# First modulation in two halves of the features, with projection work between them, and x loaded first

## What is computed

```python
def modulation(c, w, b):
    return jnp.split(jax.nn.silu(c) @ w + b, 3, axis=-1)

def sandwich(x, mod, g_pre, g_post, fn):
    shift, scale, gate = mod
    h = rms_norm(x, g_pre) * (1.0 + scale[:, None]) + shift[:, None]
    return x + gate[:, None] * rms_norm(fn(h), g_post)
...
u, qr, fr, vr, gr = jnp.split(h @ hyb_w_in[j], split_at, axis=-1)
```

## Time and profile before

| | us |
|---|---|
| median of three runs | 1368.7 |
| lowest and highest run | 1366.57, 1370.73 |
| the profiled execution | 1364.06 |
| its span in the trace | 1362.3 |

### The profile page before, as it was taken

How to read it: one execution, slowest core, us unless ns; L and a number is a source line. 1 busy time by engine, 2 the same in 40 slices (tenths; PEclk the granted TensorE clock), 3 DMA queues, 4 the chain that set the end, 5 groups by cost and what they waited for, 6 DMA issues and landing times.

```text
span 1362.3 us, 22480 instructions
## 1 busy us (share of the span) xinstructions
PE 1337.2 (98%) x8896; PEld 1210.6 (89%) x8896; DVE 867.1 (64%) x1135; ACT 721.1 (53%) x1070; POOL 50.2 (4%) x76
## 2 busy tenths in 40 slices
PE   9999899999999999999999999999999998999999
PEld 8998699999789879999999899889999896899997
DVE  5788878886798557555565666564455567644554
ACT  3575554444644456444456663655555666655553
POOL 0101000000111000000001000000000000000000
PEclk7899899999899998999999999999999999999999
DMA  9978679985599633555555443355555542355540
GB/s 351 332 294 285 225 241 314 309 309 187 201 353 364 220 65 124 186 185 185 187 183 191 155 161 124 125 185 186 186 188 187 180 165 79 126 190 193 185 154 31
DMA packets 146337, 275.54 MB, mean 202 GB/s; under 512 B 4727, under 2 KB 83343, under 8 KB 146136
## 3 DMA queue, kind: packets, MB, share of 16 engines
q1 hardware_dynamic: 131152, 220.21, 47.9%
q0 software_dynamic: 13872, 52.05, 11.4%
q10 hardware_dynamic: 1240, 2.26, 0.5%
HBM read 273.40 MB, written 1.10 MB: 202 GB/s over the span
## 4 chain that ended last, share of the span: by engine, by line
PE 92%; DVE 4%; ACT 2%; issue 1%; DMA 1%; ACTq 0%; DVEq 0%
PE ps L1946 89%; PE ps L2084 1%; DVE acc_a L1193 1%; DVE wlo L1180 1%; PE ps L2315 1%; DMA ada_ring<-in_ada_w 1%; ACT whi L504 1%; DVE xn L1294 0%; ACT xn L558 0%; PE ps L2415 0%; DVE x L1281 0%; DVE h L1273 0%; DVE x L1288 0%; ACT small L565 0%; DVE hlo L1880 0%
## 5 line engine op out<-in xcount | busy, mean ns | idle before, releaser
L1180 DVE TENSOR_TENSOR wlo<-raw,whi 128x1024 fp32r<-128x1024 f32 x400 | 485.5, 1223 | 363.0 <-ACT whi L504 361.9
L504 ACT CAST whi<-raw 128x1024 fp32r<-128x1024 f32 x400 | 417.6, 1051 | 479.6 <-PE ps L1946 471.0
L1946 PE MATMUL ps<-hhi,whi 128*128 128x256 f32 x1792 | 507.0, 283 | 2.0 <-DVE hlo L1341 1.6
L1946 PE MATMUL ps<-hhi,wlo 128*128 128x256 f32 x1792 | 500.5, 279 | 0.0
L1946 PE MATMUL ps<-hlo,whi 128*128 128x256 f32 x1792 | 500.0, 279 | 0.0
L1946 PEld LDWEIGHTS ps<-hhi,whi 128*128 128x128 f32 x1792 | 336.1, 188 | 7.7 <-issue 5.1
L1946 PEld LDWEIGHTS ps<-hlo,whi 128*128 128x128 f32 x1792 | 336.1, 188 | 4.5 <-issue 2.2
L1946 PEld LDWEIGHTS ps<-hhi,wlo 128*128 128x128 f32 x1792 | 336.5, 188 | 0.0
L1946 PE MATMUL ps<-whi,hidhi 128*128 128x512 f32 x432 | 170.3, 394 | 0.0
L1946 PE MATMUL ps<-wlo,hidhi 128*128 128x512 f32 x432 | 169.1, 391 | 0.0
L1946 PE MATMUL ps<-whi,hidlo 128*128 128x512 f32 x432 | 168.7, 391 | 0.0
(11 more groups left out here) (234 smaller groups left out, 1181.9 us busy)
## 6 DMA issues: line engine op xcount, KB each, us to landing
raw<-in_ffn_w_in SPq DMA_DIRECT2D x44, 1024.0 KB, 6.0
ada_ring<-in_ada_w POOLq DMA_DIRECT2D x40, 1024.0 KB, 7.1
raw<-in_w_mlp_up SPq DMA_DIRECT2D x32, 1024.0 KB, 5.4
raw<-in_w_mlp_down SPq DMA_DIRECT2D x32, 1024.0 KB, 4.9
raw<-in_ffn_w_out SPq DMA_DIRECT2D x22, 1024.0 KB, 4.9
raw<-in_att_w_qkv SPq DMA_DIRECT2D x18, 1024.0 KB, 6.4
raw<-in_w_in_even SPq DMA_DIRECT2D x18, 1024.0 KB, 5.0
raw<-in_hyb_w_in SPq DMA_DIRECT2D x10, 1024.0 KB, 9.7
```

What stands on the lines that cost most here:

```text
L504: A.copy(whi[:, H % 4, :], raw[:, slot(n), h * HALF:(h + 1) * HALF]).then_inc(s["hi_ready"], 1)
L1180: V.tensor_tensor(wlo[:, H % 4, :], raw[:, slot(n), h * HALF:(h + 1) * HALF], whi[:, H % 4, :].bitcast(F32), ALU.subtract).then_inc(s["lo_ ...
L1946: return pe.matmul(out, lhsT, rhs, start=first, stop=last, skip_group_check=True)
```

## The change

Four things are different.

1. SP loads x first, then modulation loads 0 to 3, then the first 512 rows of projection blocks 0 and 1, then modulation loads 4 to 7, then the other rows of the two blocks. The modulation loads are put in another order of columns, so that the first four hold shift and scale of features 0 to 511, and the other four those of features 512 to 1023. The positions in the ring of slots follow (`ADA_POS`, `HYB_POS`).
2. `mod_first(0)` forms shift and scale of features 0 to 511 after four loads. ACT and DVE then make chunks 0 to 3 of `h`, and TensorE does halves 0 and 1 of blocks 0 and 1. Modulation loads 4 to 7 are worked on between these, then `mod_first(1)` forms the other features, and halves 2 and 3 of both blocks follow. The blocks now lie in PSUM banks 0 and 4, the third in 2, since two blocks are open at a time; the column sums move to banks 2 and 3.
3. On ACT the norms of x and the normalised x come ahead of the copies of the tables, and the three constant loads (`masks`, `bandqk`, `poolw`) ahead of the chunks of the second half of the features. On DVE `mean_x` comes ahead of the modulation.
4. On TensorE the transposes move from behind the sixth modulation load to behind the third, and the number of warm-up products is another at each place (`warm_cols` is `warm_ones` into another bank).

The core of the diff:

```diff
+            if b in (1, 2):
+                return (4, 2)[b - 1]
...
+        ADA_POS, HYB_POS = (0, 1, 2, 3, 6, 7, 8, 9), (4, 5, 10, 11)
...
+            def vacated(p):
+
+                if p in ADA_POS:
+                    sp.wait_ge(s["ada_used"], ADA_POS.index(p) + 1)
+                    sp.wait_ge(s["ada_pe"], ADA_POS.index(p) + 1)
+                elif p >= 0:
+                    sp.wait_ge(s["lo_ready"], 2 * HYB_POS.index(p) + 2)
...
-            for a in range(ADA_FIRST):
-                load(a - ADA_FIRST, 0, src_cols(t["ada_w"][0, 0], (a // 2) * 512, a % 2))
-                if a == 3:
-                    sp.dma_start(x[:, :, :], t["x"][0].rearrange("(t p) n -> p t n", p=P)).then_inc(s["x_in"], 16)
-            proj(FIRST["hyb_in"], t["hyb_w_in"][0], HYB)
+            sp.dma_start(x[:, :, :], t["x"][0].rearrange("(t p) n -> p t n", p=P)).then_inc(s["x_in"], 16)
+            for a in range(4):
+                load_ada(a)
+            for b in range(2):
+                load(b, 0, src_cols(t["hyb_w_in"][0], HYB[b][1], 0))
+            for a in range(4, ADA_FIRST):
+                load_ada(a)
+            for b in range(2):
+                load(2 + b, 0, src_cols(t["hyb_w_in"][0], HYB[b][1], 1))
+            proj(FIRST["hyb_in"] + 4, t["hyb_w_in"][0], HYB[2:])
...
+            mean_x(0, 0)
+            mean_x(0, 1)
             for a in range(4):
                 ada_first(a)
-            mean_x(0, 0)
-            mean_x(0, 1)
-            for a in range(4, ADA_FIRST):
-                ada_first(a)
-            mod_cols(0, 0)
+            mod_first(0)
+            shifted(0, 1)
             split(0)
-            pre(0)
+            low(0, 0)
+            low(0, 1)
+            shifted(0, 3)
+            split(1)
+            low(0, 2)
+            low(0, 3)
+            ada_first(4)
+            split(2)
+            ada_first(5)
+            split(3)
+            ada_first(6)
+            ada_first(7)
+            split(4)
+            mod_first(1)
...
-            for a in range(1, ADA_FIRST):
-                ada_cols(a)
-                warm_ones(2)
-                if a in (3, 5):
-                    add_cols(a // 2 - 1)
-                if a == 5:
-                    pe.wait_ge(s["vec_dil_c"], 4)
-                    turn(0)
-                if a == 6:
-                    add_cols(2)
+            warm_ones(4)
+            ada_cols(1)
+            warm_ones(4)
+            add_cols(0)
+            ada_cols(2)
+            pe.wait_ge(s["vec_dil_c"], 4)
+            turn(0)
+            ada_cols(3)
+            warm_ones(6)
+            add_cols(1)
+            warm_ones(12)
+            for h in range(2):
+                proj_half(HYB[0][0], pair_of(0), h, h, 0, 0)
+            ada_cols(4)
+            proj_half(HYB[1][0], pair_of(1), 2, 0)
+            ada_cols(5)
+            add_cols(2)
+            proj_half(HYB[1][0], pair_of(1), 3, 1)
+            ada_cols(6)
+            ada_cols(7)
+            warm_cols(4)
             add_cols(3)
-            warm_ones(12)
-
-            proj("hyb_in", HYB[0:2], j=0)
+            warm_cols(8)
+            for h in range(2, 4):
+                proj_half(HYB[0][0], pair_of(0), h + 2, h, 0, 0)
+            for h in range(2, 4):
+                proj_half(HYB[1][0], pair_of(1), h + 4, h)
```

More of the change, by code:

```diff
@@ L619, in pre @@
+                    chunk(j, k)
                     for H in splits_after(j, k):
@@ L687, in _ @@
             act.wait_ge(s["one_ready"], 1)
+            norms(0)
+            for tt, lo, hi in ((0, 0, D), (1, 0, 256), (1, 256, D)):
+                act.wait_ge(s["root_x"], tt + 1)
+                act.wait_ge(s["ssq_x"], 2 * tt + 2)
+                A.activation(xn1[:, tt, lo:hi], x[:, tt, lo:hi], ACT.Copy,
+                             scale=small[:, 5, 3 + tt:4 + tt]).then_inc(s["xn_ready"], 1)
             for g in range(3):
@@ L715, in _ @@
             act.dma_start(poolw[:, :, :], t["pool_w"][0].rearrange("g c d -> c g d")).then_inc(s["band_in"], 16)
+            split(4)
+            split(5)
+            act.wait_ge(s["mod_ready"], 2)
+            for i in range(4, KD):
+                chunk(0, i)
+            for H in range(6, 10):
+                split(H)
+            evac(0, 6, *HYB[0][::2], f1, tok1)
+            split(10)
+            split(11)
+            evac(1, 8, *HYB[1][::2], f1, tok1)
             fl = f1[:, :, :].rearrange("p a b -> p (a b)")
-            for b in range(3):
-                proj("hyb_in", HYB[b:b + 1], f1, tok1, b)
+            for b in range(1, 3):
+                if b == 2:
+                    proj("hyb_in", HYB[b:b + 1], f1, tok1, b)
                 if b == 1:
@@ new lines, in low @@
+            def low(j, k):
+                lo, hi = hlo[:, k, :], hhi[:, k, :].bitcast(F32)
+                if j < 4:
+                    dve.wait_ge(s["hhi_ready"], 8 * j + k + 1)
+                    V.tensor_tensor(lo, h32_slot(j, k), hi, ALU.subtract).then_inc(s["hlo_ready"], 1)
+                else:
+                    dve.wait_ge(s["hhi_ready"], 8 * j + bank_last(j, k) + 1)
+                    V.scalar_tensor_tensor(out=lo, in0=turned_ps(j, k), scalar=scol[:, j, k:k + 1], in1=hi,
+                                           op0=ALU.mult, op1=ALU.subtract).then_inc(s["hlo_ready"], 1)
@@ L2155, in warm_ones, with warm_cols @@
                     mm(ps[:, 1, 0:P], ones[:, :], ones[:, :])
+            def warm_cols(n):
+                for _ in range(n):
+                    mm(ps[:, 2, 2 * P:3 * P], ones[:, :], ones[:, :])
             def ada_cols(a):
-                pe.wait_ge(raw_in[a % RAW], 16 * (a // RAW + 1))
+                ada_raw_in(pe, a)
                 for kk in ada_direct(a):
```

144 lines of the change are left out of this document (85 added, 59 removed).

## The result

The change makes the kernel slower by half a per cent. Over 20 runs of each side, its median is 1374.66 us against 1368.21 us, and the ratio is 1.0048 with a 95% interval of 1.0035 to 1.006. The forecast was 1369.2 in a range of 1362.5 to 1376.0. The range holds the result, but the likeliest case (no measurable change) does not: the kernel came 5.5 us later than it said and lost by more than 0.3%. As a difference to the kernel before, +0.5 us was forecast and +6.45 measured.

What follows compares the result with a forecast made beforehand. It took TensorE's own list of small work, partly at half clock, as the bound. Terms of -1.5, +1 (gate weights) and +1 (clock fall) gave +0.5 us on the median 1368.7: 1369.2, range 1362.5 to 1376.

Steps and rivals of the forecast that it cites:

- the likeliest case: Whole kernel: no change beyond about 0.3% (4.1 us) against before; chance 0.52.
- The path is TensorE's list: First 66 us: TensorE's own gapless list of small work, not the loads, sets the time.
- Comes back with the transposes: Early stretch: clock falls behind the table products, returns to full with the transposes; block two ends 64.45 against 65.98.
- Rival (b): Early stretch: only the twelve warm-ups restore the clock, not the transposes; +3.2 us, +5.2 with allowances; chance 0.17.
- Idle time ahead of the first group, 1.74 us: TensorE at 8.96: waits for the first modulation load, now usable at 10.70; 0 to 1.74 us, taken as 1.74.
- rival (c): Start: new idle time at 8.96 drops the clock before the table products; +3.6 us, about +5.6 with allowances; chance 0.08.
- Gate weights, "I allow 1": Behind block two: gate weights begin some 3 us before its end, lateness partly covered; 0 to 6 us, allowed 1.
- the ring: Gate-weight loads behind block two: each later load is requested when its buffer is read, so late use delays later loads.
- rival (d): Block two's end to 120: late gate weights make VectorE, then TensorE, wait; +5 to +6 us; chance 0.05.
- The clock behind the fourth half, "I allow 1": Low groups after the fourth half: the clock may fall there; nothing up to 2.5 us, allowed 1.
- The sum: Whole kernel: -1.5 early, +1 gate weights, +1 clock fall gives +0.5 us, put on the median: 1369.2.

Runs made afterwards that it cites:

- second execution of before: The kernel before, unchanged, profiled once more: 1368.72 us.
- second execution of after: The kernel after, unchanged, profiled once more: 1373.08 us.
- part 3: Two runs on start idle time: x loaded first in the kernel before, ratio 1.0057; 30 start warm-up products instead of 24 in the kernel after, 1.0006.
- early gate weights: Kernel after with the first gate loads requested after the fourth modulation load and used earlier on VectorE: 1373.31 us, ratio 1.0038.
- the pair of executions at their medians: Both kernels unchanged, one profiled execution each, near their medians: before 1368.72 us, after 1374.64 us.
- moved gate block: Without the 14 warm-up products, 30 at the start, first gate block ahead of ninth and tenth low halves, against the kernel after: 1362.67 us, ratio 0.9976.

## Why the prediction was right and wrong

- **The path is TensorE's list: right.** The early times of the profiled execution follow from counts and the two levels of the clock, and its only other idle time up to block two's end is 0.23 us, for VectorE, ahead of the fifth half. A slip of reading did no harm: 0.67 in 16:17 puts the first fall at 16.3, not at 16.7, and the time at half clock before is 23.9 us, so up to 12 us lost, not 11.
- **"Comes back with the transposes": wrong, the step that failed early.** Rival (b), which held against it, gave first columns at 33.64, first projection 38.76 and block two's end 69.2. Measured are 34.31, 38.43 and 69.53, and half clock at 32 was its sign. That the last two agree so closely is partly luck: the columns came 0.7 later, the clock rose before the end of the twelve warm-up products and saved 1.0, and the rest took 0.6 longer. The forecast gave it 0.17 because the trace showed a rise at 33.4. The error was to read a rule from one rise in one execution. Of the 14 profiled executions of all versions, the clock came back inside the transposes or within 0.7 us of their end in seven, stayed at half past them in six, and had not fallen in one. The Trainium skill ("TensorE: Matmul & The Clock Gate", Part 4: PE-mode transpose) says that the full clock doesn't engage for products in transpose mode. Six of these executions fit it, but seven speak against it, if these transposes run in that mode, which the record does not say. What decides between the two stays open.
- **Idle time ahead of the first group, 1.74 us: about right in size (1.53), wrong in weight.** It was priced as time only, with 0.08 for rival (c), the clock falling with it. That fall came in three of the four profiled executions with an idle time of 1.4 us or more (1.93, 1.44 and 1.98, not 1.53), and in none of the ten others, five of them with 0.79 to 1.27 and five with none. The three are also executions whose warm-up products went over to full speed early (last section). But so are the second execution of before, with no idle time there, and two of those with 30 products at the start (0.83 and 0.84 us). These had no such fall, so the idle time is the likelier cause. By the medians of part 3 the start is worth some 6 us in either direction.
- **Gate weights, "I allow 1": too small, and the largest miss.** The start of the first gate block was right ("some 3 us ahead of the end", measured 3.2). What was wrong is that its lateness would be covered. It cost 2.15 us by level 1 (3.25 - 1.10) and some 1.5 of the 2.4 more by the second transposes, so 3.6 to 4.5 us in place of 1. The rows that the prediction read end at 110, and it weighed only the wait of 1.30 in them. Further on, in the same trace of before, the ring makes VectorE wait 4.09 and 0.81 us (at 126.44 and 130.10), so a delay there is not covered. The upper bound of 6 us held. The sign of rival (d), idle time of TensorE ended by VectorE between block two and 120, came (1.99 us at level 1). Its price of 5 to 6 us, given 0.05, is nearer to the measured one than the allowance of 1.
- **The clock behind the fourth half, "I allow 1": about right.** It cost nothing in the first execution of after and 1.1 us in the second. Its upper bound of 2.5 was nearly right too: 2.7 in one execution with the early gate weights. With late loads on top it cost 7.6 us (block two's end 70.30 against 59.81, less the 2.85 by which the first projection was later already), which no bound of the prediction held.
- **The sum.** It put the difference, +0.5, on the median of before as if both kernels drew the same early clock. By the pair of executions at their medians, block two's end is +1.1 and not -1.5, the fall behind the fourth half is 0 and not +1, and what follows, most of it the ring, is +4.5 and not +1. That gives 5.6 of the 6.45 us measured. That the range held the result owes to its width, which took in the rivals. The halves themselves seem to win: x first alone costs 4 us at block two's end, the whole change only 1.1. This is not shown. It is a difference of single executions, whose clock paths alone move block two's end by 2.5 us, and no run had the halves without x first.

## What to carry to other kernels

A ring that asks for its next load when the last is read turns a late first use into a late chain, so count what each later load waits for before moving that use, and do not ask early where the same DMA engines carry loads that are due sooner. Fill idle time ahead of small work with products that cost nothing there, and try the kernel without them where they lie on the path. Before a rise or a fall of the clock is given a cause, look at a second execution.

## What the runs showed that was not expected

- The clock's path is not fixed by the program. With the same code, the kernel before was first back at full at 33.4 in one execution and at 45.3 in another; the kernel after at 37.4 in one, and at 14.9 and again at 28.5 in the other (the first rise, during the warm-up products of the start, is not counted here). The Trainium skill ("TensorE: Matmul & The Clock Gate", Part 1) says that the same kernel shows different counts of slow products at its start from run to run. The runs here agree, and show it for the later falls and rises too, at a cost of microseconds; the prediction had not weighed it.
- The 24 warm-up products of the start end at 8.96 in one execution of before and 8.15 in another (start of the next row), though the granted clock reads 1.00 in all windows from 1.5 us on in both. The counts of rows show what the clock column does not: TensorE has 6 or 7 rows in a window of 1 us at first and 11 to 13 later. The count is 11 from 6:7 on in the one and from 5:6 on (9 in 4:5) in the other, so the start runs at about half speed in both, and for longer in the one. Why the turn comes at another time stays open. With an early end the wait for the first load is longer, and the three executions whose clock fell at once are among those with an early turn.
- Between the second and the third transposes the list takes 197.6 to 198.7 us in six executions and 199.9 to 200.1 in the eight others, with nothing between; the two executions of before fall on either side. What differs is the clock: it is at half for 2.8 to 4.0 us behind the start of the second transposes in the six and for 8.5 to 9.3 in the eight. That alone is 1.2 to 2.5 us of scatter, and it hid the gain of the moved gate block.
